# Both groups of heads of the last prompt tile on 128 partitions, and its inputs and the first cache pages fetched earlier

## The reference, cut to what matters

```python
def _diff_attn(q, k, v, pos_q, pos_k, lam, table):
    s = jnp.einsum('bqhgcd,bkhcd->bhgcqk', q, k).astype(jnp.float32) * A_DH ** -0.5
    bias = jnp.transpose(_t5_bias(pos_q[:, None] - pos_k[None, :], table), (2, 0, 1))
    ...
    p = jax.nn.softmax(jnp.where(mask, s + bias, -jnp.inf), axis=-1)
    a = p[:, :, :, 0] - lam * p[:, :, :, 1]
    o = jnp.einsum('bhgqk,bkhe->bqhge', a.astype(v.dtype), v)
```

## Time and profile before

| | us |
|---|---|
| median of 3 runs | 2503.56 (2503.22 to 2504.62) |
| profiled execution | 2500.09 |
| its span in the trace | 2497.8 |
| layer 0: prompt attention's last copy ends, last tile begins | 1202.9, 1203.1 |
| layer 0: first sample matmul | 1246.40 |
| layer 1: last tile begins | 2269.4 |
| layer 1: first sample matmul | 2306.31 |

### The profile page before, as it was taken

The page is one execution under the profiler, slowest core; times in us unless marked ns, Lnnn a source line. Parts: engine busy times, 40 slices in busy tenths (PEclk is TensorE's granted clock), DMA queues, the critical chain, the costliest instruction groups (busy, mean ns, idle before and its releaser), DMA issues. The chain is left out here.

```text
span 2497.8 us, 30500 instructions
## 1 busy us (share of the span) xinstructions
PE 2171.3 (87%) x9834; PEld 1300.7 (52%) x9834; DVE 1110.0 (44%) x2450; ACT 679.7 (27%) x1573; POOL 274.5 (11%) x365
## 2 busy tenths in 40 slices
PE   7999899998888877898499888967999968997898
PEld 3444466664877764566244444623654425774343
DVE  1000000543566546998212211058888876651022
ACT  3221000221333325677200111034011106652010
POOL 0000000001233301211211120030000000002320
PEclk9999999997999976999689999979999989997999
DMA  7000011000000012000453553023100011004962
GB/s 260 35 34 34 21 51 50 22 20 12 5 9 5 10 46 77 20 17 9 145 172 118 179 186 112 17 61 106 44 9 25 25 45 60 18 9 141 323 194 99
DMA packets 127125, 176.35 MB, mean 71 GB/s; under 512 B 22944, under 2 KB 96609, under 8 KB 125953
## 3 DMA queue, kind: packets, MB, share of 16 engines
q1 hardware_dynamic: 93544, 126.34, 15.3%
q0 software_dynamic: 10640, 26.15, 3.3%
q10 hardware_dynamic: 22800, 22.13, 2.8%
HBM read 146.09 MB, written 28.56 MB: 70 GB/s over the span
## 5 line engine op out<-in xcount | busy, mean ns | idle before, releaser
L554 PE MATMUL banks<-actT 128*128 128x350 f32 (+1 forms) x960 | 283.8, 459 | 7.8 <-ACTq L564 7.8
L554 PEld LDWEIGHTS banks<-actT 128*128 128x128 f32 x960 | 182.9, 191 | 107.8 <-ACTq L564 8.0
L198 PE MATMUL banks<-fr_w,actT 128*128 128x512 f32 (+1 forms) x640 | 237.1, 528 | 0.0
L481 PE MATMUL banks<-ptg_w,heads 128*128 128x512 f32 (+1 forms) x432 | 185.8, 592 | 1.7 <-ACT heads L428 1.7
L3348 DVE TENSOR_SCALAR_CACHE_REDUCE ch_hits<-c_chosen,ch_cand 128x384 bf16<-128x384 f32 (+1 forms) x186 | 175.8, 945 | 21.2 <-DVE ch_cand L3353 15.4
L198 PEld LDWEIGHTS banks<-fr_w,actT 128*128 128x128 f32 x640 | 113.2, 192 | 124.8 <-issue 124.7
L2464 PE MATMUL banks<-a_weights,actT 128*128 128x512 f32 x384 | 171.9, 605 | 0.0
L481 PEld LDWEIGHTS banks<-ptg_w,heads 128*128 128x128 f32 (+1 forms) x432 | 77.7, 180 | 109.3 <-issue 109.3
L2464 PEld LDWEIGHTS banks<-a_weights,actT 128*128 128x128 f32 x384 | 73.3, 195 | 97.9 <-issue 97.9
L1840 ACT ACTIVATE aa_prob<-aa_prob,aa_mx 128x128 f32<-128x128 f32 (+7 forms) x128 | 98.1, 767 | 95.7 <-DVE aa_mx L1941 95.7
L619 PE MATMUL banks<-actT,kv_rows 128*128 128x350 f32 (+1 forms) x384 | 120.5, 474 | 1.0 <-PEq L347 1.0
(11 more groups left out here) (528 smaller groups left out, 3477.4 us busy)
## 6 DMA issues: line engine op xcount, KB each, us to landing
tok_rows<-fr_stage SPq DMA_DIRECT2D x8, 1028.0 KB, 3.9
fr_w<-w_in_e_dram SPq DMA_DIRECT2D x8, 1024.0 KB, 23.4
c_pages<-cache_c_k_dram SPq DMA_DIRECT2D x54, 128.0 KB, 3.2
a_pages<-cache_a_k_dram POOLq DMA_DIRECT2D x50, 128.0 KB, 3.4
a_pages<-cache_a_k_dram SPq DMA_DIRECT2D x50, 128.0 KB, 3.3
c_pages<-cache_c_k_dram POOLq DMA_DIRECT2D x49, 128.0 KB, 3.5
actT<-w_in_e_dram SPq DMA_DIRECT2D x6, 1024.0 KB, 5.5
a_weights<-w_out_e_dram SPq DMA_DIRECT2D x3, 2048.0 KB, 13.2
```

What stands on the lines that cost most here:

```text
L198: last = nc.tensor.matmul(m.ps[:, j, 0:g[1]], m.actT[:, c, t * P:t * P + P], weights[j][:, c, :], start=(c == 0), stop=(c == KC - 1))
L481: last = nc.tensor.matmul(m.ps[0:r, j, 0:g[1]], rows[:, slot, c, 0:r], weights[j][:, c, :], start=(c == 0), stop=(c == KC - 1))
L554: last = nc.tensor.matmul(m.ps[:, NS * j + k, 0:tn], wring[:, s, c, j * P:(j + 1) * P], m.actT[:, c, t0:t0 + tn], start=(c == 0), stop=(c ...
```

## The change

The last tile's block works on both groups at once: R becomes 128, group 0 on partitions 0 to 63 and group 1 on 64 to 127. The loop over groups stays only around single matmuls (scores, selection, values), which are written in turn for the two halves of the partitions. VectorE's and ScalarE's steps, the transposes and the copies run once on 128 partitions. The product with the values begins when the first of three copies is done. Bias and gates come from a new object, `LastTile`: it loads them with 64 small transfers on SyncE's queue (each of 4 rows) in `prompt_attention`, behind the gates of tile 3. In layer 0 the first 16 cache pages follow there, all on SyncE's queue, and the last tile's block keeps only the gain and the weights. In layer 1 the first 2 MB of output weights follow there, and the pages stay in the last tile's block, ahead of nothing but the small `sel` load.

```diff
-def prompt_attention(nc, m, tok, diff, out_gain, outs):
+def prompt_attention(nc, m, tok, diff, out_gain, outs, loads):
...
                     if p.t == 2:
                         store_kv(sp, m, outs)
+                    if p.t == 3:
+                        loads(sp)
...
-        self.EARLY_SP, self.EARLY_POOL = range(0, per // 2), range(per // 2, per)
+        self.EARLY_SP, self.EARLY_POOL = range(0, early or per // 2), range(early or per // 2, per)
...
+class LastTile:
...
+    def load(self, sp, tok):
+        for r in range(TAIL):
+            for n in range(KV):
+                rows = slice(n * self.R + r * G, n * self.R + r * G + G)
+                at = FAR - P - r
+                sp.dma_start(self.bias[rows], self.m.bias[n * G:n * G + G, at:at + self.NEAR]).then_inc(self.bias_in, 16)
+                c0 = TOK_G + n * G * P
+                sp.dma_start(self.gate[rows], tok[self.Q0 + r:self.Q0 + r + 1, c0:c0 + G * P]
+                             .rearrange("o (j d) -> (o j) d", j=G)).then_inc(self.gate_in, 16)
...
-    PER = 5
+    PER, PV_BANK, Y_BANK = 4, 3, 6
...
+                pe.wait_ge(s["q_ready"], KV)
+                for c in range(NC):
+                    for w0, w1 in SPANS:
+                        for n in range(KV):
+                            out = scores(c, w0, w1)[n * RG:n * RG + RG]
+                            last = nc.tensor.matmul(out, q[:, n, c, :], m.kT[:, n, w0:w1], start=True, stop=diff)
+                        if not diff:
+                            for n in range(KV):
+                                out = scores(c, w0, w1)[n * RG:n * RG + RG]
+                                last = nc.tensor.matmul(out, sel[:], m.chosen[FULL][:, w0:w1], start=False, stop=True)
+                    last.then_inc(s["scores_mm"], 1)
...
+                for b in range(NT):
+                    if b % PER == 0:
+                        pe.wait_ge(s["probs_out"], b // PER + 1)
+                    for n in range(KV):
+                        last = nc.tensor.matmul(m.ps[n * RG:n * RG + RG, PV_BANK, 0:P], probT[:, b, n * RG:n * RG + RG],
+                                                m.v[:, b, n * P:n * P + P], start=(b == 0), stop=(b == NT - 1))
+                last.then_inc(s["pv_mm"], 1)
...
-                dve.wait_ge(s["bias_in"], 16 * TAIL)
+                dve.wait_ge(tile.bias_in, 16 * KV * TAIL)
...
+            ring = PageRing(m, io["cache_a_k"], io["cache_a_v"][0].rearrange("n t a b -> n t (a b)"), 2, "sa", 8, 8)
+
+            def first_loads(sp):
+                tile.load(sp, m.tok)
+                for u in range(ring.slots):
+                    ring.load_unit(sp, u, ring.EARLY_SP, ring.unit_in)
...
+            def first_loads_1(sp):
+                tile.load(sp, m.tok1)
+                sp.dma_start(last_weights(m)[0], io["w_out_o"][0].rearrange("(c p) n -> p c n", p=P)[:, 0:4, :])\
+                    .then_inc(po1_in[0], 16)
```

183 lines of the change are left out of this document (79 added, 104 removed).

## The result

The changed kernel takes 2488.15 us (median of 4 runs, 2485.29 to 2490.36), the kernel before beside it 2503.39 us (4 runs, 2502.97 to 2504.62). The ratio is 0.9938 with an interval of [0.992, 0.9955]: faster by 15.2 us, where 29.2 were forecast. The profiled execution of the change took 2490.36 us, its span is 2488.7. That of before took 2500.09, so the two profiles differ by 9.7 us only, and their stages can't be added up to the difference of the medians.

A forecast was written before the change was run, and what follows sets the result against it. In the last tile's block a chain of dependent steps, not an engine, was taken as the bound. Gains of 19.0 + 6.6 + 3.6 = 29.2 us gave 2474.4 us as the forecast, 2467 to 2484 for 8 in 10.

The forecast's parts named there:

- Layer 1's last tile: Layer 1's last-tile block ends with GpSimd's last page issue, 2297.88 instead of 2304.53: 6.6 us gained.
- The cost is nothing: Small loads and pages moved into layer 0's attention take 40 us of SyncE's queue, ahead of tile 4's gates: no cost.
- The shorter wait of layer 1's samples: At layer 1's sample block TensorE waits 5 us for the `kv_rows` weights instead of 8.80: 3.6 us gained.
- rival without overlap: Pairs of passes on the two partition halves don't overlap, in scores and value product: 2486.8 us; 10 in 100.
- Layer 0's last tile, steps 1 to 6: Queries, scores, bias, transposes, value product, way to the first sample matmul, which comes 19.0 us sooner (17.5 to 20.5).
- The moved loads: 64 small loads and 16 pages on SyncE in layer 0's attention, 64 and one in layer 1: no cost.
- No gate came late: Rival: tile 4's gates come late in SyncE's queue in layer 0's attention, making the kernel slower; 2 in 100.

The follow-up runs named there:

- e3_split3: The changed kernel with layer 1's early pages shared by three queues, GpSimd 17 instead of 24: 2481.87 us, ratio 0.9914 to the kernel before.
- e1_again: The changed kernel unchanged, run once more: 2485.98 us beside 2503.72 for the kernel before, ratio 0.9931.
- e14_wait_all: e8_race_wait with GpSimd's wait for VectorE's mix at every tile instead of tile 1 alone: 2472.7 us, ratio 0.9876 to the kernel before.
- e4_tile_only: The changed kernel without loads in the prompt attention; bias, gates, pages and weights load in the last tile's block: 2507.79 us, ratio 1.0026 to the kernel before.
- e8_race_wait: The changed kernel with pages on three queues, ten idle VectorE memsets, and GpSimd's multiply at tile 1 waiting for VectorE's mix: 2474.08 us, ratio 0.9879.
- e2: The changed kernel with ten idle one-column VectorE memsets in layer 0's last tile: 2484.9 us, ratio 0.9925 to the kernel before.
- e10: The changed kernel with only GpSimd's wait for VectorE's mix at tile 1 added: 2487.46 us, ratio 0.9932 to the kernel before.
- e13: The changed kernel with five idle one-column VectorE memsets ahead of its work in layer 0's prompt attention: 2482.15 us, a single time.

## Why the prediction was wrong

The steps that failed are these. Layer 1's last tile was taken to end with GpSimd's last issue, 6.6 us sooner; it ends with the drain behind it, and gave 2.7. "The cost is nothing" stood for everything outside the two tiles and the samples; the attention lost 3.2 to 5.3 us to a race that the loads don't cause, and the key search 3.5. The shorter wait of layer 1's samples was counted in full, 3.6 us; 0.8 to 1.9 arrived at the fourth unit. That the median, 2488.15, lies beside the 2486.8 of the rival without overlap is chance: the pairs do overlap, and the loss is elsewhere.

**Layer 0's last tile, steps 1 to 6: right.** 19.0 us forecast; against the 43.3 of before in the mean it gave 20.9 in the profile of the result and in e3_split3, and 18.6 to 19.9 in the others of the table that keep the early loads. Single steps: scores 5.43 forecast, 5.32 measured; transposes 2.4 and 2.18; the product 4.1, with 3.8 as its lower bound, and 2.60, 3.33 (e1_again) and 3.06 (e14_wait_all). I had read the 0.21 us of a pass at the low clock as its floor; in the records a pair takes 0.21 at the low clock, as a single pass did, and 0.11 at the high one, and the 2.60 us are four steps at the one and 14 at the other. The rival of pairs that don't overlap is dead: at either clock a pair takes the time of a single pass, and its two passes start 3 to 7 ns apart. So is, for this case, the rule cited for it from the Trainium skill, TensorE: Matmul & The Clock Gate, on packing small matmuls: 36 loads and 36 passes over the same 128 rows and two halves of the columns fit into 2.60 us, with each load's record beside a running pass.

**The moved loads: their price was right, the stage's was not.** No gate came late (VectorE's products with the gates wait for no transfer in the changed kernel, and e4_tile_only has the same attention without the loads). But the attention takes 3.2 to 5.3 us more. Where it takes 5.3 more, the tile behind it takes 22.4 us, and where it takes 3.2 more, 24.7; the sum is 283.0 to 283.3 us in the five of the table that have both the early loads and the race. So the two stages give 15.4 us and not 19.0. The mechanism is the race (e8_race_wait, e14_wait_all), tipped by ten nanoseconds whose source is open. No rows ahead of the prediction could size it, but the same profile held its pattern: GpSimd's multiply with 2.32 us at one place and 1.90 at seven, and a VectorE instruction of 2.35 us among ones of 0.75.

**Layer 1's last tile: wrong by its own step.** "So the block ends with GpSimd, 2297.88 instead of 2304.53: 6.6 us." The stream was the right one, its end was not: the drain behind the last issue takes 3.8 us more. With it the sum gives 2304.5 - 2301.1 = 3.4. The two profiles of the result have 3.3 (36.9 and 33.6); against the mean of the five of before, 36.2, it is 2.7. This is the term that a second look at the block's end in the earlier trace rows would have mended: what comes behind the last issue is part of the stream.

**Layer 1's samples: right in its mechanism, too large in its size.** With S again the block's first issue, the wait for the weights ends at S + 15.3 in the profile of the result, and at S + 13.6 to 15.8 in the five profiles that have the early weights and the unshared pages (after, e1, e2, e10, e13); in the five of before it ends at S + 17.3 to 18.5. So the weights do land some 3 us sooner. But I left the keys ahead of them at S + 8.5, and they end at S + 9.4 to 9.7, since the clock has fallen in the 13 us in which TensorE waits for GpSimd: the time that I called hidden isn't without a price. The fourth unit's keys start 0.8 us sooner in the two profiles of the result, and 1.9 sooner in the means of five and five (S + 26.03 for S + 27.98; the five with the change scatter over 3 us), where the forecast had 3.6. The turn-taking rule of the Trainium skill (DMA: Bandwidth & Descriptors, arbitration) would have the weights land at S + 15.4, and my own working had S + 13.6; the profiles lie between the two and beyond, and don't decide.

**What the sum left out: the search.** 3.5 us, gone when five or ten of the ten instructions of VectorE that the tile no longer has are put back as idle ones. The forecast counted these instructions as time saved in the block and didn't ask what lies behind them in the program.

Put together: 15.4 + 2.7 + 1.9 - 3.5 = 16.5 us, where the medians gave 15.2 and 17.7. This agreement leaves out the stretch from the samples to the index scores; with the 3.5 us that it is longer in the mean (below) the sum would be 13.0. The range of 2467 to 2484 took in the bounds of each priced term and no loss in a stage that the change leaves alone. With the losses mended and the pages shared by three queues the same change takes 2472.7 to 2480.3 us.

**Open.** Why ten nanoseconds differ at the custom instruction between before and the change, when VectorE's code up to there has the same instructions in the same order. Buffers, semaphores, the moved loads and ten later instructions are ruled out; how the program is laid out in memory wasn't tried apart. Nor does a run show why one place of the code costs more than another. And the stretch of the samples and index scores takes 488.2 us in the mean of six profiles without the change (484.6 to 491.8) and 491.7 of fourteen with it (488.8 to 493.7): the ranges overlap and the clock differs between executions of one kernel, but of the 84 pairs of one without and one with the change the one with it is longer in 73. So chance alone is an unlikely reason, and no run here shows the cause.

## What to carry to other kernels

A stream that issues loads ends when its drain ends, so read the drain's row at the block's end before calling another stream the longest. Where an instruction of VectorE has a few records of several times its usual length, look for one of GpSimd that starts within some tens of nanoseconds, and order the two by a wait on GpSimd's side: here that was worth 6 us of an attention, more than layer 1's whole part of the change. Time in which TensorE waits behind another stream isn't free: the next block can start at the low clock. And a change in the number of instructions moves the code of every loop behind it; when a stage that wasn't touched moves by an even amount each turn, pad and look again.

## What the runs showed of the hardware

- Two engines that meet: a mix of 0.62 us takes 2.35 beside a GpSimd multiply of 1.90, or the multiply takes 2.32 beside the mix of 0.62. Where the mix's record started 51 to 58 ns ahead of the multiply's (four profiles) VectorE won, where it started 41 to 43 ns ahead (nine profiles) it lost; small instructions are hit too (a 128x1 ratio took 1.54 us instead of 0.22).
- The place of code: a loop's last instruction came 0.11 us later in each of 31 turns with ten instructions fewer ahead of it, and a single hold of 130 to 142 ns moved forward with five instructions more.
- GpSimd's drain behind its last page took 3.8 us in layer 1 before and 3.9 after, against 0.84 in layer 0 where it had issued none; where the records tell the last page's landing, the drain ended 0.4 to 1.0 us behind it.
- Two passes of 128 columns on the two halves of the output partitions, each with its own weights, together took 0.21 us at the low clock and 0.11 at the high one, as one pass alone.
- After 13.5 us without a matmul the granted clock of the next 8.2 us was 0.67 in the mean and the same 48 passes took 7.99 us; after 2.1 us it was 0.80 and they took 6.95.
- Four profiles of one kernel differ by 3.5 us in one stretch of 484.6 to 488.1 us, with a granted clock of 0.91 to 0.90 in it.
